# Sparse attention of one block by pairs of heads: scores of two heads in turn, z projection in halves, output projection begun among the last heads, fewer transposes

## The reference, cut to what matters

```python
def nsa_shared_kv(stream, kv_norm_g, kv_w, ...):
    s = rmsnorm_2(stream, kv_norm_g)
    kv = (s @ kv_w).reshape(Bn, T, 6, B_GROUPS, B_HEAD_DIM).transpose(2, 0, 3, 1, 4)
...
    def compress(tok, pos, w1, w2):
        blk = tok[:, :, idx] + pos            # 15 blocks of 32 tokens, stride 16
        return jax.nn.silu(blk.reshape(Bn, B_GROUPS, n_cmp, L_CMP * B_HEAD_DIM) @ w1) @ w2
...
def nsa_layer(h, shared, rel_bias, in_w, out_w):
    proj = h @ in_w
    z = proj[..., B_WIDTH:4 * B_WIDTH].reshape(Bn, T, N_BRANCH, B_HEADS, B_HEAD_DIM)
    gates = jax.nn.sigmoid(proj[..., 4 * B_WIDTH:].astype(jnp.float32)).reshape(Bn, T, N_BRANCH, B_HEADS)
...
        s_c = jnp.einsum('bghqd,bgcd->bghqc', qb, k_cmp).astype(jnp.float32) + dense_bias(d_c)
        p_c = masked_softmax(s_c, d_c >= 0)
        o_c = jnp.einsum('bghqc,bgcd->bghqd', p_c.astype(v_cmp.dtype), v_cmp)
...                                            # o_s, o_w: the same with the selected and window keys
    y = jnp.sum(gates[..., None].astype(o.dtype) * o * jax.nn.silu(z), axis=2)
    return y.reshape(Bn, T, B_WIDTH) @ out_w
```

## Time and profile before

| what | value |
|---|---|
| median of 3 runs | 1346.24 us (1344.84 to 1346.62) |
| the profiled execution | 1345.99 us, its span 1344.4 us |
| PE busy | 1317.2 us, 98% of the span |
| DVE, ACT, POOL busy | 42%, 21%, 4% |
| chain that ended last | 93% PE |
| clock granted to PE | 0.997 of full speed |

### The profile page before, as it was taken

The page is one execution under the profiler, slowest core; times in us unless marked ns, Lnnn a source line. Parts: engine busy times, 40 slices in busy tenths (PEclk is TensorE's granted clock), DMA queues, the critical chain, the costliest instruction groups (busy, mean ns, idle before and its releaser), DMA issues.

```text
span 1344.4 us, 17087 instructions
## 1 busy us (share of the span) xinstructions
PE 1317.2 (98%) x7096; PEld 1121.0 (83%) x7096; DVE 559.9 (42%) x1477; ACT 287.9 (21%) x835; POOL 49.5 (4%) x53
## 2 busy tenths in 40 slices
PE   7999999999999999999999999999999999899997
PEld 5888888986778888889888888988889998577777
DVE  4546440250046424533645641267653231165543
ACT  2100000131133443003000000333224210044441
POOL 0000000000110000010000001001000000000010
PEclk9999999999999999999999999999999999999999
DMA  9988855541613545576888774542233615522301
GB/s 327 294 294 280 300 185 172 186 159 63 250 63 133 198 160 191 196 251 232 299 295 300 263 234 140 183 157 94 66 103 108 209 41 184 147 83 64 126 1 32
DMA packets 178987, 237.46 MB, mean 177 GB/s; under 512 B 11516, under 2 KB 117294, under 8 KB 178910
## 3 DMA queue, kind: packets, MB, share of 16 engines
q1 hardware_dynamic: 175632, 230.19, 51.0%
q10 hardware_dynamic: 2542, 3.01, 0.7%
q0 software_dynamic: 736, 3.17, 0.7%
HBM read 234.89 MB, written 4.61 MB: 178 GB/s over the span
## 4 chain that ended last, share of the span: by engine, by line
PE 93%; DVE 2%; SPq 2%; DMA 1%; ACT 1%; issue 0%; POOL 0%; DVEq 0%; ACTq 0%
PE ps L191 89%; PE ps L194 3%; SPq L227 2%; DMA arena<-in_w_ada 1%; DVE tmpB L206 1%; DMA slots<-in_w_down 0%; ACT arena L197 0%; DVE tmpA L206 0%; ACT tmpC L197 0%; DVE U L206 0%; DVE rstd L218 0%; DVE H L206 0%; DVE arena L206 0%; POOL arena L200 0%; ACT tmpB L197 0%
## 5 line engine op out<-in xcount | busy, mean ns | idle before, releaser
L191 PE MATMUL ps<-U,slots 128*128 128x256 f32 (+2 forms) x3488 | 718.2, 365 | 1.2 <-ACT U L197 0.6
L191 PEld LDWEIGHTS ps<-U,slots 128*128 128x128 f32 (+1 forms) x3488 | 618.3, 190 | 83.5 <-issue 4.1
L191 PE MATMUL ps<-arena,slots 128*128 128x256 f32 (+1 forms) x1840 | 325.0, 338 | 1.7 <-DMA slots<-in_w_down 1.0
L191 PEld LDWEIGHTS ps<-arena,slots 128*128 128x128 f32 x1840 | 292.0, 191 | 32.3 <-issue 1.4
L206 DVE SCALAR_TENSOR_TENSOR tmpA<-slots,sm,tmpA 128x512 f32<-128x512 f32 x182 | 139.4, 766 | 5.9
L197 ACT ACTIVATE tmpC<-ps 128x256 f32<-128x256 f32 (+3 forms) x89 | 36.7, 416 | 409.8 <-PE ps L191 403.2
L197 ACT ACTIVATE arena<-ps 128x512 f32<-128x512 f32 (+3 forms) x118 | 50.5, 454 | 171.1 <-PE ps L191 152.7
L191 PE MATMUL ps<-arena 128*128 128x64 f32 (+8 forms) x560 | 83.9, 310 | 1.8 <-ACT arena L197 1.8
L191 PEld LDWEIGHTS ps<-arena 128*128 128x128 f32 (+2 forms) x560 | 66.0, 183 | 19.9 <-issue 13.3
L206 DVE SCALAR_TENSOR_TENSOR tmpC<-tmpC,ps 128x256 f32<-128x256 f32 (+2 forms) x48 | 19.6, 408 | 141.4 <-ACT tmpC L197 141.3
L197 ACT ACTIVATE tmpC<-H 128x512 f32<-128x512 f32 (+1 forms) x32 | 16.3, 520 | 258.6 <-DVE H L206 250.1
(11 more groups left out here) (152 smaller groups left out, 771.0 us busy)
## 6 DMA issues: line engine op xcount, KB each, us to landing
slots<-in_w_ada SPq DMA_DIRECT2D x14, 2048.0 KB, 7.8
slots<-in_w_in SPq DMA_DIRECT2D x14, 2048.0 KB, 8.2
slots<-in_ada_w SPq DMA_DIRECT2D x12, 2048.0 KB, 7.9
slots<-in_w_down SPq DMA_DIRECT2D x16, 1408.0 KB, 6.7
slots<-in_w_gate SPq DMA_DIRECT2D x19, 1024.0 KB, 5.2
slots<-in_w_up SPq DMA_DIRECT2D x19, 1024.0 KB, 7.9
slots<-in_a_in_w SPq DMA_DIRECT2D x6, 2048.0 KB, 9.0
slots<-in_b_in_w SPq DMA_DIRECT2D x12, 1024.0 KB, 5.7
```

Of the source, the lines that this page charges most:

```text
L191: return Nothing() if self.e is None else self.e.matmul(*a, **k)
```

## The change

Ahead of the loop the compression streams 30 columns against 128-column weights, so its result comes out transposed already and `t_cmp2` falls away (the factor 0.5 moves into `v_cmp3`). Its products stand between those of q pairs 2 and 3. The gates are made likewise, between the products of z block 1, without `t_ng_turn`. Two z blocks stand ahead of the loop, not three. The `cw` loads move ahead.

The loop has ten steps of a pair of heads. The scores of the two heads alternate product by product; the z block is cut into halves, one between scores and mixes, one behind the transposes (`ZIN` lists which block stands in which step); mixes are two steps behind the scores, transposes one. The two transposes of the compressed branch become one of 47 columns (columns 775 to 799 are zero). `EE` has a fourth buffer. The output projection of pair 0 over heads' columns 0 to 5 (`t_bo`) stands in step 8, pair 1 behind step 9, and then both over columns 6 and 7.

```diff
+            for s in range(2):
+                fetch("cw", s)
             fetch("z", 0)
             fetch("kv", 1)
-            for n in (1, 2):
-                fetch("z", n)
-            for s in range(2):
-                fetch("cw", s)
             fetch("ng", 0)
...
-            for m in range(16):
-                i = e.matmul(ps[0:30, 0:T], BLK[:, s, m, :, :].rearrange("p g n -> p (g n)"), wv[:, m, :], start=m == 0, stop=m == 15)
...
+            for j in range(2):
+                o = pair * 256 % 512 + j * P
+                for k in range(8):
+                    i = e.matmul(qp[:, j * T:(j + 1) * T], wq[:, k, o:o + P], U[:, k, :], start=k == 0, stop=k == 7)
...
+                    for m in (2 * k, 2 * k + 1):
+                        i = e.matmul(ps[:, 30 * j:30 * j + 30], wv[:, m, j * P:(j + 1) * P], BLK[:, s, m, :, :].rearrange("p g n -> p (g n)"),
...
+        def t_z_ng(e, n):
...
+            for j in range(2):
+                for k in range(8):
+                    i = e.matmul(zp[:, j * T:(j + 1) * T], wz[:, k, j * P:(j + 1) * P], U[:, k, :], start=k == 0, stop=k == 7)
...
+                    i = e.matmul(ps[:, 48 * j:48 * j + 48], U[:, k, j * P:(j + 1) * P], wv[:, k, :], start=k == 0, stop=k == 7)
...
+        LZ = ring(banks[2][:, :], banks[0][:, :])
+        PS = ring(*[banks[b][:, :] for b in (3, 4, 5, 1)])
...
+            hs = (2 * t, 2 * t + 1)
...
+            for h in hs:
+                pa, free = PS.open("na a", h)
...
+                e.matmul(pa[:, 0:256], q[h % 2][:, 0:128], kx[h % 2][:, 0:542].rearrange("p (b t) -> p b t", b=2)[:, :, 0:128])
+            for h in hs:
+                e.matmul(ps[h % 2][:, 256:512], q[h % 2][:, 128:256], kx[h % 2][:, 0:256]).then_inc(*pe.up("na a", h))
...
+                e.matmul(pb[:, 15:286], q[h % 2][:, 128:256], kx[h % 2][:, 256:527])
+            for h in hs:
+                e.matmul(ps[h % 2][:, 0:7], q[h % 2][:, 0:128], kx[h % 2][:, 256:263]).then_inc(*pe.up("na b", h))
...
+                if b:
+                    e.wait_ge(*dve.at("na p", h, 2))
+                    i = e.transpose(ps[0:47, 384:512], E[:, 768:815], ident)
...
+        ZIN = [(2,), (3, 4)] + [(t + 3,) for t in range(2, 9)]
...
+            t_nq_cmp1(e, 2, 0)
+            t_nq_cmp1(e, 3, 1)
+            t_linear(e, "z", 0, U, u_in("n5"), 256, ("z", 0))
+            t_cmp3(e, 0)
+            t_kv(e, 4)
+            for i in range(2):
+                t_kv_tokens(e, 1, i)
+            t_cmp3(e, 1)
+            t_z_ng(e, 1)
+            for x in free_of(L) + free_of(X):
+                e.wait_ge(*x)
+            for t in range(10):
+                if t < 8:
                     t_na_scores(e, t)
+                if t < 9:
+                    t_z_half(e, ZIN[t][0], 0)
+                if t == 1:
+                    t_z_half(e, ZIN[t][0], 1)
+                if t >= 2:
+                    t_na_mix(e, 2 * t - 4)
+                    t_na_mix(e, 2 * t - 3)
+                if 1 <= t < 9:
+                    t_na_turn(e, 2 * t - 2)
+                    t_na_turn(e, 2 * t - 1)
+                if t == 1:
+                    t_z_half(e, ZIN[t][1], 0)
+                if t < 9:
+                    t_z_half(e, ZIN[t][-1], 1)
+                if t == 8:
+                    t_bo(e, 0, range(0, 6))
+            t_bo(e, 1, range(0, 6))
+            t_bo(e, 0, range(6, 8))
+            t_bo(e, 1, range(6, 8))
...
+            for t in range(10):
+                if t < 8:
+                    v_na_scores(e, 2 * t)
+                    v_na_scores(e, 2 * t + 1)
+                if t >= 1:
+                    v_silu(e, "z", ZIN[t - 1][-1], z_dst(ZIN[t - 1][-1]), LZ)
+                if t < 8:
+                    v_na_weights(e, 2 * t)
+                    v_na_weights(e, 2 * t + 1)
...
+                if 2 <= t < 8:
+                    v_na_mix(e, t - 2)
+            v_na_mix(e, 6)
+            v_na_mix(e, 7)
```

More of the change, by code:

```diff
@@ L835, in v_residual @@
                     dve.mark("res", n[0:2], c, h)
-            L.close([dve.now()], n, pair, *by_half(half))
+            to.close([dve.now()], n, pair, *by_half(half))
         actT = arena[:, 0:22 * T].rearrange("p (c t) -> p c t", t=T)
@@ L2086, in v_kv_tokens, with t_nq_cmp1 @@
             L.close([dve.now()], "vw", b, i)
-        def t_cmp1(e, s):
+        def t_nq_cmp1(e, pair, s):
+            qp, free = L.open("nq", pair)
+            for f in free:
+                e.wait_ge(*f)
+            e.wait_ge(*arrived("nq", 1))
             ps, free = L.open("cw", s)
@@ L2164, in z_at @@
             return dve.at("z", 3 * (j // 2) + b)
-        def t_ng(e):
+        def t_z_ng(e, n):
+            zp, free = L.open("z", n)
+            for f in free:
+                e.wait_ge(*f)
+            e.wait_ge(*arrived("z", n))
             ps, free = L.open("ng")
@@ new lines, in t_z_half @@
+        def t_z_half(e, n, j):
+            if j == 0:
+                ps, free = LZ.open("z", n)
+                for f in free:
+                    e.wait_ge(*f)
+                e.wait_ge(*arrived("z", n))
+            ps, (wv,) = LZ.buf("z", n), w_of("z", n)
+            for k in range(8):
+                i = e.matmul(ps[:, j * T:(j + 1) * T], wv[:, k, j * P:(j + 1) * P], U[:, k, :], start=k == 0, stop=k == 7)
+            if j == 1:
+                i.then_inc(*pe.up("z", n))
+                W.close([pe.now()], "z", n)
@@ L2327, in t_na_mix, with t_bo @@
             EA.close([pe.now()], "na", h)
+        def t_bo(e, pair, ks):
+            if 0 in ks:
+                ps, free = LZ.open("bo", pair)
+                for f in free:
+                    e.wait_ge(*f)
+                e.wait_ge(*arrived("bo", 0))
+            ps, (wv,) = LZ.buf("bo", pair), w_of("bo", 0)
+            for j in range(2):
+                o = pair * 256 + j * P
+                for k in ks:
+                    e.wait_ge(*pool.at("yn", k))
+                    i = e.matmul(ps[:, j * T:(j + 1) * T], wv[:, k, o:o + P], YN[:, k, :], start=k == 0 and j == 0, stop=k == 7,
+                                 skip_group_check=True)
+            if 7 in ks:
+                i.then_inc(*pe.up("bo", pair))
+                if pair == 1:
+                    W.close([pe.now()], "bo", 0)
         def v_na_mix(e, j):
@@ L2562, in tensor @@
-            e.wait_ge(*act.at("na turn", 15, 1))
-            e.wait_ge(*dve.at("na y", 7, 1))
-            yn = lambda k, half: pool.at("yn", k)
-            for pair in range(4):
-                t_linear(e, "bo", pair, YN, yn, half=0 if pair >= 2 else None)
-            t_linear(e, "bo", 2, YN, yn, half=1)
+            for j in range(3):
+                t_kv(e, j)
+            for i in range(2):
+                t_kv_tokens(e, 0, i)
+            t_nq_cmp1(e, 2, 0)
+            t_nq_cmp1(e, 3, 1)
@@ L2773, in vector @@
+            v_blocks(e, 1)
+            v_keys(e, 0)
+            for i in range(2):
+                v_kv_tokens(e, 0, i)
+            v_cmp1(e, 0)
+            v_cmp1(e, 1)
+            v_silu(e, "z", 0, z_dst(0))
+            v_cmp3(e, 0)
+            v_keys(e, 1)
+            for i in range(2):
+                v_kv_tokens(e, 1, i)
+            v_cmp3(e, 1)
+            v_silu(e, "z", 1, z_dst(1))
             v_ng(e)
-            for n in range(3):
-                e.memset(EE.bufs[n][:, 775:783], 0.0).then_inc(*dve.up())
+            for n in range(4):
+                e.memset(EE.bufs[n][:, 775:800], 0.0).then_inc(*dve.up())
@@ L2790, in vector @@
                     for pair in (2, 3):
[L2791 removed]
+                        v_residual(e, "bo", pair, mods[:, 112:120], "n5", 1, LZ)
                 v_root(e, "no", half)
```

200 lines of the change are left out of this document (72 added, 128 removed).

## The result

The changed kernel takes 1326.9 us (median of 4 runs; the profiled execution 1324.96), the kernel before 1346.4: a ratio of 0.9844 (0.9811 to 0.9876). The forecast was 1327.6. The profiled execution of before has a short stretch at half clock, long ahead of the code that is changed; that of after has none there. (Both end with some 4 us at half clock after PE's last pass, which is left out of account.) A stretch of 3.4 us at half clock does the work of 1.7, so it costs 1.7 us.

What follows compares the result with a forecast made beforehand. PE, busy 98% of the span, was taken to bound the kernel; -13.3 - 2.9 + 1.4 - 1.3 - 5.2 + 2.7 = -18.6 us took the profiled 1345.99 to 1327.4, forecast as a 1327.6 us median, range 1324.5 to 1330.5 (chance 0.68).

Steps and rivals of the forecast that it cites:

- scores: In the loop, alternating two heads' score products would take 1.70 us a pair, 13.6 in all instead of 26.9: -13.3 us.
- transposes: In the loop, 14 passes a pair in 1.59 us, 12.7 in all instead of 15.6: -2.9 us.
- z in halves: In steps 2 to 8, seven z blocks cut by a mix of another shape, each with an extra entry and exit: +1.4 us.
- mixes: In the loop, the mixes would stay as they were, 16 x 2.02 us.
- end of the loop: PE's waits of 0.40, 0.29 and 0.59 us around the last two mixes would be covered by moved work: -1.3 us.
- ahead, removed: Ahead of the loop, two stretches of transposes and waits of 1.80 us and the gates' 1.60 would go: -5.2 us.
- ahead, passes: Ahead of the loop, compression passes 7.2 us a side instead of 6.9, gates 3.6 instead of 3.5: together +0.7 us.
- ahead, waits: Two new waits for PSUM banks, 1.5 us before the loop's first scores and 0.5 before q pair 3's products.
- the rival of half the overlap: Loop scores: each pair costs 2.71 us as heads 0 and 1 did, +8.1 us, 1335.7 us; chance 0.09.
- The other, that changing row sets costs a drain: Loop scores: each row-set switch costs 0.2 us and nothing overlaps, 11.2 plus 14.1 us, 1352.9 us; chance 0.03.
- The rival of 1321.6: Loop mixes: one head's last four passes lie beside the next head's first, -6.0 us, 1321.6 us; chance 0.06.
- the rival of 1316.4: Ahead of the loop: short passes' weight loads hide under 256-column passes, -11.2 us, 1316.4 us; chance 0.04.

Runs made afterwards that it cites:

- the run at 1328.03: Changed kernel with the output projection of pairs 0 and 1 whole behind the last mixes: its lowest run, 1328.03 us; the kernel measured 1334.37 us.

## Why the prediction was right, step by step

| step | predicted | measured, and where |
|---|---|---|
| scores | -13.3 | 26.9 - 8 x 1.64 = -13.8; the third row of the loop less the second |
| transposes | -2.9 | 8 x 1.59: -2.9; with eight a head again, +1.7 in the step, +1.8 in the time |
| z in halves | +1.4 | (3.55 + 3.65 - 7.01) x 7 = +1.3; whole again, -1.1 |
| mixes | 0 | 4.03 a pair against 2 x 2.02: 0 |
| end of the loop | -1.3 | no wait left: -1.3 |
| ahead, removed | -5.2 | no transpose and no such wait left; by the rows of before -5.2 |
| ahead, passes | +0.7 | a group 0.88 us = 2 x 0.216 + 4 x 0.112, a gate group 0.66: +0.7 |
| ahead, waits | +2.0 | 1.36 + 0.37: +1.7 |
| sum | -18.6 | -19.5, where the stretch as a whole gave -19.6 |

A check by stretches: up to the first scores 86.1 us before, with four z blocks, and 69.8 after, with two; less two blocks of 6.9 that is 2.5 us won, where the table has 2.8. From there to the end 17.1 are won, where the table has 16.7. So single rows of the table are good to some 0.4 us.

**Scores.** The number came by a sound argument and a misread row. The prediction took the order of the earlier trace rows for the alternating one. It is grouped as well: `t_da_scores` of the kernel before gives PE both products on rows 0 to 63 and then both on rows 64 to 127, four passes and four. All the same two passes have started within 0.03 us (window 381.83 to 381.86):

```profile
381.83 0.39 PE L191 MATMUL ps<-arena 64*128 64x128 f32 x2
```

So rows 5 did not show how PE treats alternate order. Together with the earlier trace rows, where groups of eight overlapped in part only, they show how far it looks ahead: past four passes of one set to the other, not past eight. That alternating puts both heads within this reach was the prediction's own argument, and it held: 1.64. Grouped in eights, would have given 2.71, and that kernel measured 2.61; the rival of half the overlap was a true statement on another order. The other, that changing row sets costs a drain, falls with 1.64 against 3.18 on one set. I took 1.70 where 1.64 came; that is the largest miss of the sum, 0.5 us.

**Waits.** Both waits were foreseen with their places, the first at 1.5 (1.36 came), the second at 0.5 (0.37), each from a pass's end, a hand-over and a duration of the earlier trace rows. Taking both away gave 1.9.

**End of the loop.** The prediction said of the moved `t_bo` that without it the 1.3 us would be back. This step was too small: 2.56 us of wait come back, not 1.3. It is another wait than those ahead of the mixes in the earlier trace rows: there PE waited for ACT's copies, here for the mix banks, which DVE frees only behind the silu of the last z block. And in six of ten runs the clock takes more, in the profiled one 5.1 us. The sum didn't hang on it, the remark did.

**Further overlap.** The rival of 1321.6 supposed that the written order lets the two mixes meet. They did not, at 4.03, not even at the seam, where grouped scores save some 0.6 us. At that seam stands the 15-row product of another shape, which was the prediction's reason against it; no run takes it away, so the reason is not shown. The row that the rival quoted, 64-column weights on two column sets in the earlier trace rows, has four passes on one set and then four on the other, side by side, and pointed to more: in turn, the mixes run side by side too, and bring 16 us, not the 6 of that rival. The Trainium skill, TensorEngine Tiling (Array Packing), Key Properties, that tiles operate independently, is borne out by the rows of equal starts (1231.90 and 1231.91), where the passes stand in turn.

**Weight loads.** A group of two long and four short passes took 0.88, which is the sum of its parts, and in coarse order a short pass costs 0.109. So interleaving hides nothing of the short passes, and the rival of 1316.4 falls.

**The base.** The sum went from the profiled 1345.99, which holds the short half-clock stretch, and so belongs with the upper level after: 1345.99 - 19.6 = 1326.4, where the runs show 1326.9. The profiled execution after, 1324.96, is without it.

## What to carry to other kernels

Where two products use different halves of the rows or of the columns, write them in turn, product by product, and read the overlap from start to start. In groups of four passes the scores of this kernel overlapped fully, in groups of eight by less than half, and the grouped mixes not at all. Read a row's program order in the kernel before building on it: the trace shows starts, not the order in which they were asked for. A wait or a long row of short passes on TensorE is to be priced with the clock behind it, not by its own length alone; here, long passes among short ones kept the clock up. Before comparing two single runs, look for a stretch at half clock in only one of them.

## What the runs showed of the hardware

- Mixes of two heads on two column sets, in turn, start within 0.01 us of each other and take 2.03 us a pair instead of 4.03, with one PSUM bank as target. On row sets 16 passes take 1.64 in turn, 2.61 grouped, 3.18 on one set.
- In program order PE reached past four passes of one row set to start the other set's within 0.03 us (381.83); of eight passes it first ran four alone, for 0.97 us (1240.65 to 1241.62).
- The granted clock fell to half with PE busy all the time, during rows of 64 passes of 30 columns (0.50 for 10.2 and 13.6 us). With two 256-column passes to every four short ones it stayed at 1.00. What exactly the chip weighs remains open.
- The same happens in the untouched layers, in some executions and not in others: behind 24 passes of one column before had 3.4 us at half clock, after none behind the same row. In the profiled run of the mixes in turn PE is busy for 44.2 of the 44.3 us at half clock from 998.9 on.
- One wait of 2.56 us was followed by 10.2 us at half clock in the profiled run; the run at 1328.03 paid for the wait alone. The waits of 1.36 and 0.37 had none behind them.
- A change of tile shape costs 0.1 us each way: seven cuts, with an entry and an exit each, cost 1.3 us as read in the rows and gave back 1.1 when taken away.
